# A streaming-encoder block: conditioning vector summed from row blocks of its weights, and a first FFN stage without the shift

## The chip, the core and the metric

The kernel runs on one core of a Trainium2 chip. The time is device microseconds of that core, from start to end of one execution. The core has TensorE (matmuls, written PE in the profile), VectorE (DVE), ScalarE (ACT), GpSimd (POOL) and SyncE (SP), which here only issues transfers. They run side by side and wait for each other by semaphores.

## The reference

A block of a network on x with 512 tokens of width 1024. A vector `ada` of 9 x 1024 numbers is made from the condition c; it gives a shift, a scale and a gate to each of three sublayers: a gated FFN, a mixer of 16 attention heads, and a second FFN.

```python
cond = jax.nn.silu(c)
ada = (cond @ w_ada[l] + b_ada[l]).reshape(b, N_SUBLAYERS, 3, D_MODEL)
shift, scale, gate = ada[:, :, 0], ada[:, :, 1], ada[:, :, 2]
h = modulate(x, g_ffn1[l], shift[:, 0], scale[:, 0])   # rmsnorm(x, g) * (1 + scale) + shift
x = x + 0.5 * gate[:, 0][:, None, :] * swiglu(h, w_ffn1_up[l], w_ffn1_down[l])
...
# swiglu(h, w_up, w_down): gate, up = split(h @ w_up); (silu(gate) * up) @ w_down
```

All is float32: x is 2 MB, `w_ada` is 37.7 MB (1024 x 9216), an FFN has 2816 hidden columns.

## The kernel before

The width of 1024 is 8 chunks of 128 rows (`KC`), on the partitions. A weight tile is 1024 rows by 128 columns, 512 KB. Precise products are made of three matmuls: each operand is split in a high part (rounded, by ScalarE: `split_hi`, `split_first`) and a low part (the remainder, by VectorE: `split_lo`, `split_first_lo`), and `three` adds high x high, high x low and low x high. So h is two tensors, `h_hi` and `h_lo`. A pair of up tiles (gate and up columns of the same 128 hidden ones) gives two PSUM banks; ScalarE takes silu of one, VectorE multiplies (`hidden`), and the product is split again.

**The start.** SP loads x in halves, eleven small vectors between the halves into `vecs`, and then sixteen column tiles of `w_ada` (shift and scale of the first sublayer, one by one for each chunk) with the first four up tiles among them. TensorE transposes x by chunks (L734); ScalarE copies and squares; VectorE sums the squares. A column of `ada` is made from a column tile in one of three ways (`ADA_ROLE`): by TensorE alone ("P": eight matmuls of one column, L712), or by a product with the condition on VectorE or GpSimd (L481), a reduce on VectorE (L1341) and one matmul with ones (L716). ScalarE adds the bias (L1069) and makes the factor `amp` (L1072). For each chunk k, VectorE normalises (L1372), ScalarE adds the shift and rounds (L1049), VectorE makes the low part (L1378), and TensorE then runs chunk k of all four first tiles (`first_tiles`, lines 688 to 690): the chunk can't start before its own shift and scale are there.

**The loop of FFN 1.** Twenty pairs, two tiles each (`up_pair`). With each pair two column tiles of `w_ada` are loaded into `ada_w`, multiplied on GpSimd (L481), reduced on VectorE (L1341) and summed over partitions on TensorE (L723). The down projection (8 output chunks) takes the last sixteen columns along.

**What sets the order.** Each engine has one queue, written by hand, and does its instructions in that order. A load of tile t waits until tile t - 4 has been split; the split of tile t waits until TensorE has used tile t - 2.

## Time and profile before

| | us |
|---|---|
| median of 3 runs | 1182.02 |
| lowest and highest | 1178.54, 1183.63 |
| span of the profiled execution | 1185.1 |
| TensorE busy in it | 1142.3 |
| VectorE, ScalarE, GpSimd busy | 650.4, 446.4, 188.5 |

The profile comes from one execution of its own. It has the busy time of every engine, the granted clock of TensorE, and for each instruction its start, its duration and what it waited for. A TensorE duration includes the pipeline's tail, so the step from one start to the next says what a matmul costs in a row of them. A float32 matmul of one column and a transpose are counted by instructions: a matmul of 128x1 has two of them.

### The profile page before, as it was taken

How to read it: one execution, taken by the hardware profiler on the slowest of the kernel's cores; microseconds unless marked ns; L12 is line 12 of the kernel's file. 1: busy time of each engine (PE TensorE's matmuls, PEld its weight loads, DVE VectorE, ACT ScalarE, POOL GpSimd, SP SyncE). 2: the span in 40 equal slices, each digit the busy share in tenths (PEclk: the TensorE clock that was granted, in tenths of full speed). 3: DMA queues.
4: the chain of work that ended last, by engine and by line, in shares of the span. 5: the costliest groups of instructions: out<-in, count | busy, mean ns of one | idle time of the engine just before them, and what ended most of it. 6: DMA issues, size and time to landing. Idle time of an engine off the chain costs nothing.

```text
span 1185.1 us, 14961 instructions
## 1 busy us (share of the span) xinstructions
PE 1142.3 (96%) x5249; PEld 915.5 (77%) x5249; DVE 650.4 (55%) x784; ACT 446.4 (38%) x748; POOL 188.5 (16%) x112
## 2 busy tenths in 40 slices
PE   7799999999999988999999999989999999999998
PEld 6678888888888865888778777777888888887876
DVE  3967676767665645566765566654333333334343
ACT  4233233232322224565676565343222222222322
POOL 2523333232322220000000000000000000225250
PEclk7699999999999998999999999999999999999999
DMA  9656666666675551112212111231333333223231
GB/s 272 156 146 175 190 172 190 173 187 168 166 183 149 149 150 36 54 54 54 54 53 64 44 36 54 61 101 52 89 96 99 88 88 100 86 72 107 83 104 71
DMA packets 231861, 131.20 MB, mean 111 GB/s; under 512 B 5148, under 2 KB 224396, under 8 KB 231820
## 3 DMA queue, kind: packets, MB, share of 16 engines
q1 hardware_dynamic: 231820, 130.66, 39.5%
q8 instruction: 25, 0.41, 0.1%
q14 instruction: 16, 0.13, 0.0%
HBM read 128.54 MB, written 2.10 MB: 110 GB/s over the span
## 4 chain that ended last, share of the span: by engine, by line
PE 89%; DVE 5%; ACT 2%; issue 1%; SPq 1%; DMA 1%; POOL 0%; DVEq 0%; ACTq 0%; POOLq 0%
PE bank L688 29%; PE bank L690 27%; PE bank L689 27%; PE bank L904 1%; PE bank L929 1%; DVE w_lo L1333 1%; PE bank L884 1%; DVE h_lo L1378 1%; DVE tmp L1372 1%; DVE ada_acc_first L1341 1%; ACT w_hi L1019 1%; SPq L608 1%; PE bank L723 1%; DMA ada_first<-in_w_ada_dram 1%; DVE w_lo L1383 1%
## 5 line engine op out<-in xcount | busy, mean ns | idle before, releaser
L1333 DVE TENSOR_TENSOR w_lo<-w_raw,w_hi 128x1024 fp32r<-128x1024 f32 x164 | 225.5, 1376 | 368.9 <-ACT w_hi L1019 367.8
L688 PE MATMUL bank<-h_hi,w_hi 128*128 128x512 f32 x864 | 353.7, 409 | 12.5 <-DVE h_lo L1378 8.0
L1019 ACT ACTIVATE w_hi<-w_raw 128x1024 fp32r<-128x1024 f32 x164 | 173.7, 1059 | 463.8 <-PE bank L690 448.3
L690 PE MATMUL bank<-h_hi,w_lo 128*128 128x512 f32 x864 | 345.0, 399 | 0.0
L689 PE MATMUL bank<-h_lo,w_hi 128*128 128x512 f32 x864 | 345.0, 399 | 0.0
L688 PEld LDWEIGHTS bank<-h_hi,w_hi 128*128 128x128 f32 x864 | 164.8, 191 | 55.2 <-DVE h_lo L1378 8.4
L689 PEld LDWEIGHTS bank<-h_lo,w_hi 128*128 128x128 f32 x864 | 164.8, 191 | 40.1 <-issue 2.6
L690 PEld LDWEIGHTS bank<-h_hi,w_lo 128*128 128x128 f32 x864 | 164.4, 190 | 40.1
L580 POOL TENSOR_TENSOR w_raw<-w_raw,gate_row 128x1024 f32<-128x1024 f32 (+1 forms) x24 | 54.9, 2287 | 662.8 <-DMA w_raw<-in_w_ffn_down_dram 662.4
L481 POOL TENSOR_TENSOR ada_w<-ada_w,cond 128x1024 f32<-128x1024 f32 x57 | 110.2, 1934 | 263.6 <-DMA ada_w<-in_w_ada_dram 263.4
L1341 DVE TENSOR_REDUCE ada_acc<-ada_w 128x128 f32<-128x1024 f32 x56 | 111.7, 1995 | 0.0
L688 PE MATMUL bank<-w_hi,hid_hi 128*128 128x512 f32 x176 | 70.4, 400 | 3.0 <-DVE w_lo L1333 3.0
L688 PE MATMUL bank<-hid_hi,w_hi 128*128 128x512 f32 x176 | 71.1, 404 | 0.3 <-DVE w_lo L1333 0.3
L690 PE MATMUL bank<-hid_hi,w_lo 128*128 128x512 f32 x176 | 69.7, 396 | 0.0
L689 PE MATMUL bank<-hid_lo,w_hi 128*128 128x512 f32 x176 | 69.7, 396 | 0.0
L690 PE MATMUL bank<-w_hi,hid_lo 128*128 128x512 f32 x176 | 69.4, 395 | 0.0
L689 PE MATMUL bank<-w_lo,hid_hi 128*128 128x512 f32 x176 | 69.0, 392 | 0.0
L1445 DVE TENSOR_TENSOR hid_lo<-tmp_b,hid_hi 128x512 f32 (+1 forms) x44 | 41.4, 946 | 36.3 <-ACT hid_hi L1105 36.3
L1105 ACT ACTIVATE hid_hi<-tmp_b 128x512 f32 (+1 forms) x44 | 27.8, 632 | 77.9 <-DVE tmp_b L1441 77.9
L1638 DVE TENSOR_TENSOR_SCAN tmp_b<-tmp_a,tmp_b 128x512 f32<-128x512 f32 (+3 forms) x32 | 25.1, 815 | 36.7 <-ACT tmp_a L1253 36.7
L688 PEld LDWEIGHTS bank<-w_hi,hid_hi 128*128 128x128 f32 x176 | 33.0, 188 | 11.4 <-DVE w_lo L1333 3.9
L690 PEld LDWEIGHTS bank<-w_hi,hid_lo 128*128 128x128 f32 x176 | 33.0, 188 | 8.5
(185 smaller groups left out, 1430.6 us busy)
## 6 DMA issues: line engine op xcount, KB each, us to landing
w_raw<-in_w_ffn_up_dram SPq DMA_DIRECT2D x88, 512.0 KB, 4.5
ada_w<-in_w_ada_dram SPq DMA_DIRECT2D x60, 512.0 KB, 3.9
w_raw<-in_w_ffn_down_dram SPq DMA_DIRECT2D x36, 512.0 KB, 4.6
w_raw<-in_w_in_dram SPq DMA_DIRECT2D x28, 512.0 KB, 3.9
ada_first<-in_w_ada_dram SPq DMA_DIRECT2D x12, 512.0 KB, 7.4
w_raw<-in_w_out_dram SPq DMA_DIRECT2D x8, 512.0 KB, 3.7
w_raw<-in_w_ffn_down_dram SPq DMA_DIRECT2D x8, 384.0 KB, 5.3
x_nat<-in_x_dram SPq DMA_DIRECT2D x2, 1024.0 KB, 5.2
```

Source lines behind the costliest of these rows:

```text
L481: return engine.tensor_tensor(tile, tile, cond[:].rearrange("p (k o) -> p k o", o=1) .broadcast_to([P, KC, P]), ALU.mult)
L580: g.tensor_tensor(tile, tile, gate_row[:, :, half * 512:(half + 1) * 512] .broadcast_to([P, nk, 512]), ALU.mult).then_inc(w_gated, 1)
L608: sp.dma_start(stage(p), ada_v[:, :, a * P:(a + 1) * P]).then_inc(ada_first_in[p], 16)
L688: mm(dst, wh, xh, start=start, stop=False, skip_group_check=skip)
L689: mm(dst, wh, xl, start=False, stop=False, skip_group_check=skip)
L690: return mm(dst, wl, xh, start=False, stop=stop, skip_group_check=skip)
L1019: a(w_hi[:, s, :], w_raw[:, r, :], ACT.Copy).then_inc(w_hi_done, 1)
L1105: a(hid_hi[:, bass.ds(f, 1), :], tmp_b[:, j:j + 1, :], ACT.Copy).then_inc(hid_hi_done, 1)
L1333: v.tensor_tensor(w_lo[:, s, :], w_raw[:, r, :], w_hi[:, s, :].bitcast(F32), ALU.subtract)\
L1341: return v.tensor_reduce(acc, tile.rearrange("p k n -> p n k"), AX_X, ALU.add).then_inc(ada_red, 1)
L1445: v.tensor_tensor(hid_lo[:, bass.ds(f, 1), :], tmp_b[:, j:j + 1, :], hid_hi[:, bass.ds(f, 1), :].bitcast(F32), ALU.subtract).then_inc(hid_ ...
L1638: last = v.tensor_tensor_scan(buf[:, back], tmp_a[:, unit % 2, back], buf[:, back], 0.0, ALU.add, ALU.add)
```

## The change

The vector `ada` is now made by row blocks. A block is one of the nine 1024-column parts; for each chunk k of 128 rows, the 128 x 1024 piece is loaded, 4 KB to a partition.

- **Scale of the first sublayer.** Its eight pieces come first, behind x. TensorE makes it alone: `ada_direct`, eight matmuls of one column for each piece, placed between the transposes and behind the sum of squares. With the last three stand matmuls on constants whose result nobody reads (`warm`: 2, 2, and 12).
- **The first four tiles without shift.** h is first xT * rstd * amp (`raw_high`, `raw_low`), and the four tiles run on this, tiles 0 and 1 ahead of 2 and 3 for the first chunks, and then as pairs (`first_pair`).
- **Shift.** Its eight pieces come behind the four weight tiles. VectorE multiplies by the condition and adds up (`shift_product`, one operation a piece), and TensorE sums over partitions (`ada_columns`, eight matmuls). The shift's part of the four tiles is a product of the unsplit weights with the shift: `shift_bias`, 32 matmuls of one column in two runs. It joins as a bias in `silu_first` and `hidden_first`.
- **h with shift** is made afterwards (`scaled`, `make_h_first`, `h_low_first`) over the same `h_hi`, `h_lo`, for tile 4 on.
- **The other seven blocks.** Five in the up loop, one for four pairs, two in the down projection. VectorE does `block_product` (one operation a piece, eight a block), TensorE `ada_columns` once a block, VectorE the bias (`ada_sum`). GpSimd has no part in it any more.
- The eleven small loads go out on ScalarE's queue. The first two weight tiles have buffers of their own. The stationary operand of the forget gate is packed.

```diff
@@ sync
             load_x(0)
-            sp.wait_ge(vec_zero, 1)
...
             load_x(1)
-            for p in range(ADA0):
-                load_ada_first(p)
-                if p in (3, 7):
-                    load_up(0, T_UP1, p // 4, p // 4, True)
+            load_first_block(B_SCALE, 0, scale_in)
+            for n in range(4):
+                load_up_first(n)
+            load_first_block(B_SHIFT, 1, shift_in)
...
+            with sp.Fori(0, UP_BLOCKS) as i:
+                for q in range(4):
+                    if q == 1:
+                        sp.wait_ge(bias_summed, 2)
+                    load_up(0, T_UP1, 4 * i + 2 + q, q % 2)
+                    if q % 2:
+                        sp.wait_ge(w_used, 4)
+                        for k in range(2 * q - 2, 2 * q + 2):
+                            load_ada(i + B_LOOP, k)
@@ tensor
+            def ada_direct(block, k, landed):
+
+                pe.wait_ge(landed[k], 16)
+                for j in range(KC):
+                    last = mm(bank[4][:, j:j + 1], ada_first[:, 1 - block, k, j * P:(j + 1) * P], cond[:, k:k + 1],
+                              start=k == 0 and j == 0, stop=k == KC - 1, skip_group_check=True)
+                if k == KC - 1:
+                    last.then_inc(ada_col, 1)
+
+            def ada_columns(products, read):
+
+                pe.wait_ge(ada_mul, products)
+                pe.wait_ge(ada_out, read)
+                for j in range(KC):
+                    last = mm(bank[4][:, j:j + 1], ada_acc[:, j * P:(j + 1) * P], ones[:], start=True, stop=True)
                 last.then_inc(ada_col, 1)
...
+            def warm(n):
+
+                for _ in range(n):
+                    mm(bank[3][:].rearrange("p (b n) -> p b n", n=P), ident_bf[:],
+                       ident_bf[:].rearrange("p (o n) -> p o n", o=1).broadcast_to([P, 4, P]), start=True, stop=True)
...
-                if k == KC - 2:
+                if k == 2:
                     pe.wait_ge(consts, N_CONSTS)
                     pe.wait_ge(cond_ready, 1)
-                    for p in range(2):
-                        ada_column_first(p)
+                if k >= 3:
+                    ada_direct(B_SCALE, k - 3, scale_in)
             sum_squares(0)
+            for k in range(KC - 3, KC):
+                ada_direct(B_SCALE, k, scale_in)
+                warm(2)
+            warm(10)
...
+            def first_pair(f, k):
+
+                pe.wait_ge(raw_done, k + 1)
+                for n in (2 * f, 2 * f + 1):
+                    last = tile_chunk(T_UP1, n, k, w2_hi, w2_lo)
...
+            def shift_bias(f):
+
+                for n in (2 * f, 2 * f + 1):
+                    for k in range(KC):
+                        raw = tile8(w_first[n], 0) if n < 2 else tile8(w_raw, n)
+                        last = mm(bank[6 + f][:, n:n + 1], raw[:, k, :], ada[:, k:k + 1], start=n % 2 == 0 and k == 0,
+                                  stop=k == KC - 1, skip_group_check=True)
+                last.then_inc(bias_summed, 1)
+
+            for n in range(2):
+                for k in range(3):
+                    pe.wait_ge(raw_done, k + 1)
+                    tile_chunk(T_UP1, n, k, w2_hi, w2_lo)
+            for k in range(3):
+                first_pair(1, k)
+            for k in range(3, KC):
+                first_pair(0, k)
+            for k in range(3, KC):
+                first_pair(1, k)
+                if k == 4:
+                    ada_columns(KC, B_SCALE)
+                if k > 5:
+                    if k == 6:
+                        pe.wait_ge(ada_out, 2)
+                    shift_bias(k - 6)
@@ vector
+            def block_product(block, k):
+
+                dve.wait_ge(ada_in[k % 2], 64 * block + 16 * (k // 2) - 112)
+                ada_product(k, ada_w[:, k % 2, :], KC * block + k - KC)
...
+            def hidden_first(f):
+
+                dve.wait_ge(bias_summed, f + 1)
+                v.tensor_copy(first_bias[:, 2 * f:2 * f + 2], bank[6 + f][:, 2 * f:2 * f + 2]).then_inc(bias_col, 1)
+                dve.wait_ge(bias_col, f + 1)
```

Two places show how the order moves. The first is TensorE's queue at the program's start, before the change (L734 transposes x, L712 and L716 are columns of `ada`, L699 and L701 the sum of squares, L688 to L690 the first tiles):

```order
L734 MATMUL bank<-ident,x_nat 128x128 x20
L712 MATMUL bank<-cond,ada_w 128x1 x16
L734 MATMUL bank<-ident,x_nat 128x128 x4
L699 MATMUL bank<-ssum,ones 128x512
L701 MATMUL bank<-tmp_a,ones 128x512
L712 MATMUL bank<-cond,ada_first 128x1 x8
L716 MATMUL bank<-ones,ada_acc_first 128x1
L712 MATMUL bank<-cond,ada_first 128x1 x8
L716 MATMUL bank<-ones,ada_acc_first 128x1
L688 MATMUL bank<-h_hi,w_hi 128x512
```

And with it (L707 transposes, L680 is `ada_direct`, L671 and L673 the sum of squares, L696 is `warm`):

```order
L707 MATMUL bank<-ident,x_nat 128x128 x4
L680 MATMUL bank<-cond,ada_first 128x1 x8
L707 MATMUL bank<-ident,x_nat 128x128 x4
L680 MATMUL bank<-cond,ada_first 128x1 x8
L671 MATMUL bank<-ssum,ones 128x512
L673 MATMUL bank<-tmp_a,ones 128x512
L680 MATMUL bank<-cond,ada_first 128x1 x8
L696 MATMUL bank<-ident_bf 128x512 x2
L680 MATMUL bank<-cond,ada_first 128x1 x8
L696 MATMUL bank<-ident_bf 128x512 x2
L680 MATMUL bank<-cond,ada_first 128x1 x8
L696 MATMUL bank<-ident_bf 128x512 x12
```

The transposes and direct groups alternate five times (the last two are shown), and three more groups with `warm` stand between the sum of squares and the first tile.

The second is TensorE at the end of the four first tiles (L755 is `shift_bias`, L789 the head of the loop). Before, the loop followed the last L690 of the tiles; now:

```order
L755 MATMUL bank<-ada,w_first_87 128x1 x8
L755 MATMUL bank<-ada,w_first_88 128x1 x8
L660 MATMUL bank<-h_hi,w_hi 128x512
L661 MATMUL bank<-h_lo,w_hi 128x512
L662 MATMUL bank<-h_hi,w_lo 128x512
L660 MATMUL bank<-h_hi,w_hi 128x512
L661 MATMUL bank<-h_lo,w_hi 128x512
L662 MATMUL bank<-h_hi,w_lo 128x512
L755 MATMUL bank<-ada,w_raw 128x1 x16
L789 UNCONDITIONAL_BRANCH
```

Two runs of sixteen matmuls of one column, 32 instructions each, have come in, with one chunk of tiles 2 and 3 between.

## Rows read from the trace of the kernel before

**Rows 1.** The page: busy time, the chain that ended last, a load's landing
```profile
PE 1142.3 (96%) x5249; PEld 915.5 (77%) x5249; DVE 650.4 (55%) x784; ACT 446.4 (38%) x748; POOL 188.5 (16%) x112
...
PE 89%; DVE 5%; ACT 2%; issue 1%; SPq 1%; DMA 1%; POOL 0%; DVEq 0%; ACTq 0%; POOLq 0%
...
w_raw<-in_w_ffn_up_dram SPq DMA_DIRECT2D x88, 512.0 KB, 4.5
```
**Rows 2.** Windows: stretch, length, busy us (count) by engine, clock, DMA, GB/s
```profile
13.20:16.00 2.80, 2.80 (x28) 2.80 (x27) 1.55 (x3) 1.34 (x3) 0.00 (x0) 1.00 1.16 290
...
21.50:28.80 7.30, 7.30 (x35) 7.23 (x33) 1.93 (x3) 4.49 (x10) 1.90 (x1) 0.50 1.17 292
...
56.90:58.80 1.90, 1.90 (x19) 1.90 (x18) 1.86 (x2) 0.00 (x0) 0.00 (x0) 1.00 0.00 0
71.30:73.60 2.30, 0.14 (x2) 0.01 (x1) 2.30 (x3) 1.17 (x3) 2.12 (x2) 1.00 1.19 294
74.10:77.40 3.30, 3.30 (x9) 2.53 (x9) 3.30 (x5) 0.70 (x2) 0.60 (x1) 0.50 0.10 26
100.00:200.00 100.00, 100.00 (x446) 81.19 (x445) 70.79 (x53) 30.48 (x51) 32.29 (x17) 1.00 0.64 179
```
**Rows 3.** Timeline of TensorE, 6 to 79 us: start, duration, instruction, idle before
```profile
6.06 1.94 PE L734 MATMUL bank<-ident,x_nat 128*128 128x128 f32 x8 [6.06 <-DMA x_nat<-in_x_dram]
...
12.64 0.66 PE L734 MATMUL bank<-ident,x_nat 128*128 128x128 f32 x4 [0.32 <-ACT tmp_a L1032]
13.13 4.20 PE L712 MATMUL bank<-cond,ada_w 128*128 128x1 f32 x32
17.20 1.09 PE L734 MATMUL bank<-ident,x_nat 128*128 128x128 f32 x4
18.08 1.91 PE L699 MATMUL bank<-ssum,ones 128*128 128x512 f32 x2
...
21.50 3.41 PE L712 MATMUL bank<-cond,ada_first 128*128 128x1 f32 x16
...
34.81 0.80 PE L688 MATMUL bank<-h_hi,w_hi 128*128 128x512 f32 x1 [5.37 <-DVE h_lo L1378]
35.40 0.63 PE L689 MATMUL bank<-h_lo,w_hi 128*128 128x512 f32 x1
35.83 0.63 PE L690 MATMUL bank<-h_hi,w_lo 128*128 128x512 f32 x1
...
71.04 0.39 PE L690 MATMUL bank<-h_hi,w_lo 128*128 128x512 f32 x1
73.59 0.51 PE L688 MATMUL bank<-h_hi,w_hi 128*128 128x512 f32 x1 [2.16 <-DVE tmp_b L1441]
...
78.04 0.40 PE L688 MATMUL bank<-h_hi,w_hi 128*128 128x512 f32 x1
78.28 0.40 PE L689 MATMUL bank<-h_lo,w_hi 128*128 128x512 f32 x1
```
**Rows 4.** Timeline of ScalarE: the first table load, a weight split
```profile
0.74 1.28 ACT L1026 ACT_TABLE_LOAD   x1 [0.74 <-PEq L1712]
...
31.37 1.06 ACT L1078 ACTIVATE w_hi<-w_raw 128x1024 fp32r<-128x1024 f32 x1 [1.16 <-DMA w_raw<-in_w_ffn_up_dram]
```
**Rows 5.** Timeline of SyncE's queue: the small loads' first issue, x's second half
```profile
1.25 0.51 SPq L622 DMA_DIRECT2D vecs<-in_b_ada_dram  x1
...
5.00 0.41 SPq L611 DMA_DIRECT2D x_nat<-in_x_dram  x1
```
**Rows 6.** Timeline of VectorE: the condition's last step, h low, weight low, product
```profile
10.33 0.17 DVE L1412 TENSOR_TENSOR cond<-cond,vcol 128x8 f32<-128x8 f32 x1
...
38.35 0.73 DVE L1378 SCALAR_TENSOR_TENSOR h_lo<-tmp,ada,h_hi 128x512 fp32r<-128x512 f32 x1
39.01 1.21 DVE L1383 TENSOR_TENSOR w_lo<-w_raw,w_hi 128x1024 fp32r<-128x1024 f32 x1
...
42.00 1.21 DVE L481 TENSOR_TENSOR ada_first<-ada_first,cond 128x1024 f32<-128x1024 f32 x1
```

More of the change, by code:

```diff
@@ L24 @@
 EPS = 1e-6
-N_IDENT, N_CONSTS = 2, 15
+N_IDENT, N_CONSTS = 4, 15
 NEG = -(2.0 ** 126)
@@ L30 @@
 NADA = 9 * KC
-ADA0 = 2 * KC
-ADA_ROLE = "PPPGPGPG" "GDGGPGDG"
-ADA_DOWN = ADA0 + 2 * (FC - 2)
-ADA_SUMS = [p for p in range(ADA0) if ADA_ROLE[p] != "P"]
+NBLOCK = 9
+B_SHIFT, B_SCALE, B_LOOP = 0, 1, 2
+UP_BLOCKS = (FC - 2) // 4
+DOWN_CHUNKS = (3, 3, 2, 0)
 T_UP1 = 0
@@ L778, in up_pair @@
                     last.then_inc(w_used, 1)
[L779 to L785 removed]
+            with pe.Fori(0, UP_BLOCKS) as i:
+                for q in range(4):
+                    up_pair(T_UP1, 4 * i + 2 + q, q % 2, 0, q == 0)
+                ada_columns(KC * i + 2 * KC, i + B_LOOP)
             pe.wait_ge(hid_done, FC - 1)
@@ L1097, in up_chunk @@
                         a(tmp_a[:, j, :], bank[j][:], ACT.Silu).then_inc(silu_done, 1)
-                if with_ada:
-                    for half in range(2):
-                        ada_bias(ADA0 - 4 + 2 * f + half, half)
                 hidden_high(f, j, hid0)
@@ L1295, in _ @@
             make_h(2)
-            ffn_up(T_UP2, FC, False)
+            nc.scalar.preload_act_table_set("silu_and_others")
+            split_hi(T_UP2 + 2 * SPLIT, used=T_UP2)
+            for j in range(2):
+                act.wait_ge(w_used, T_UP2 + 2 * j + 1)
+                a(tmp_a[:, j, :], bank[j][:], ACT.Silu).then_inc(silu_done, 1)
+            split_hi(T_UP2 + 2 * SPLIT + 1, used=T_UP2 + 1)
+            for j in range(2):
+                hidden_high(j, j, FC)
+            with act.Fori(1, FC // 2 - 1) as i:
+                for j in range(2):
+                    up_chunk(T_UP2, 2 * i + j, j, FC)
+            for j in range(2):
+                up_chunk(T_UP2, FC - 2 + j, j, FC)
             def square_out(half, tb):
@@ new lines, in hidden_low @@
+            def hidden_low(f, j, hid0):
+                dve.wait_ge(hid_hi_done, hid0 + f + 1)
+                v.tensor_tensor(hid_lo[:, bass.ds(f, 1), :], tmp_b[:, j:j + 1, :],
+                                hid_hi[:, bass.ds(f, 1), :].bitcast(F32), ALU.subtract).then_inc(hid_done, 1)
+            dve.wait_ge(rstd_done, 1)
+            for k in range(KC):
+                v.tensor_tensor(xr[:, k, :], xT[:, k, :], rstd[:], ALU.mult).then_inc(xr_done, 1)
+            ada_sum(B_SCALE, 1)
+            dve.wait_ge(ada_out, 1)
@@ new lines, in _ @@
+            v.scalar_tensor_tensor(amp[:], ada[:, KC:2 * KC], 1.0, col(R_G[0], KC), ALU.add, ALU.mult).then_inc(amp_done, 1)
+            dve.wait_ge(amp_done, 1)
+            dve.wait_ge(xr_done, KC)
+            raw_low(0)
+            split_up(0)
+            raw_low(1)
+            split_up(1)
+            raw_low(2)
+            raw_low(3)
+            split_up(2)
+            raw_low(4)
+            split_up(3)
+            raw_low(5)
+            shift_product(0)
+            raw_low(6)
@@ new lines, in _ @@
+            shift_product(1)
+            raw_low(7)
+            for k in range(2, KC):
+                shift_product(k)
+            ada_sum(B_SHIFT, 2)
+            dve.wait_ge(ada_out, 2)
+            scaled(0)
+            for k in range(1, 4):
+                scaled(k)
+                h_low_first(k - 1)
+            split_lo(2 * SPLIT)
+            scaled(4)
+            h_low_first(3)
+            hidden_first(0)
+            scaled(5)
+            h_low_first(4)
+            split_lo(2 * SPLIT + 1)
@@ L1436, in hidden @@
+            for k in range(6, KC):
+                scaled(k)
+                h_low_first(k - 1)
+            h_low_first(KC - 1)
+            hidden_low(0, 0, 0)
+            hidden_first(1)
+            hidden_low(1, 1, 0)
             def hidden(base, f, j, hid0, first=False):
@@ L1678, in _ @@
             split_first_lo(T_UP2 + 2, w3_hi, w3_lo)
-            coefficients(2, 9 * KC)
+            coefficients(2)
             normed(2)
-            ffn_up(T_UP2, FC, False)
+            split_lo(T_UP2 + 2 * SPLIT)
+            for j in range(2):
+                hidden(T_UP2, j, j, FC, True)
+            split_lo(T_UP2 + 2 * SPLIT + 1)
+            for j in range(2):
+                hidden_low(j, j, FC)
+            with dve.Fori(1, FC // 2) as i:
+                for j in range(2):
+                    f = 2 * i + j
+                    for half in range(2):
+                        split_lo(T_UP2 + 2 * f + half + SPLIT, half, (2 * j + half + SPLIT) % RAW)
+                    hidden(T_UP2, f, j, FC)
+                    hidden_low(f, j, FC)
             for t in range(T_DOWN2 + SPLIT, T_DOWN2 + len(NAT_PARTS) + SPLIT):
```

401 lines of the change are left out of this document (175 added, 226 removed).

## The prediction, made before the changed kernel was run

> **What bounds the kernel now.** I read the page first, then the TensorE row of time in the first 90 us, then what the other engines and the DMA do in the same stretch. The page shows TensorE busy 96% of the span and 89% of the chain that ended last is TensorE's [rows 1], so only stretches where TensorE idles, runs at the half clock or does small extra matmuls can change the time. From 100 to 200 us, inside the up loop, it is busy without a break at the full clock, with 64% of the DMA's share in use [rows 2]; the loops are its own time. The losses are at the start, and the change works there.
>
> In that start the reader is to see five things. The first transposes start at 6.06, the first matmul of the up tiles at 34.81, the last of the four first tiles at 71.04 and the first of the loop at 73.59 [rows 3]: the 96 matmuls of the first tiles spread over 36.5 us. A 128x512 matmul follows the one before it by 0.43 us at the half clock (35.40 to 35.83) and by some 0.233 at the full one (78.04 to 78.28) [rows 3]; 96 are 22.4 us at full. The granted clock was 1.00 (2.4 GHz) up to 16.0, 0.50 (1.2 GHz) behind it, 1.00 again at 56.9, and 0.50 once more from 74.1 to 77.4, behind the idle 71.3 to 73.6 [rows 2]. A 128x1 matmul is two instructions: 19 in 1.9 us at full (56.9 to 58.8), 35 in 7.3 at half (21.5 to 28.8) [rows 2], so eight matmuls, 16 instructions, are 1.7 and 3.3. And TensorE was busy with little else for all of 13.2 to 16.0 and 21.5 to 28.8; right behind the first the clock was lost, and in the second it did not come back [rows 2, 3].
>
> **The change, part by part.** I follow TensorE's new order.
>
> Start to the third transpose group. x's second half is no longer behind eleven small loads on SP; these go out on ScalarE's queue once its table is loaded at 2.02 [rows 4]. Eleven issues took from 1.25 to 5.0 on SP [rows 5], so on ScalarE they would end near 5.8, before its first copy, which waits for the transposes of 6.06 [rows 3]. The vector of conditions is ready at 10.5 before (VectorE at 10.33) [rows 6]. I take 10.6 again; if the small loads are late behind x and the weights, each microsecond counts. TensorE then does the fourth group of transposes: 11.2.
>
> The scale block on TensorE. Eight groups of 16 instructions (ada_direct) stand there, against six such in the whole start before. Bounds: 1.7 each at full, 3.3 at half. The first two I take at full (before, the same mix kept the full clock to 16.0, [rows 2]); from then on half. Sum: 11.2 + 1.7 + 0.6 + 1.7 = 15.2; three groups of transposes at 0.9 (17.20 to 18.08; 0.6 at full, 12.64; [rows 3]) and three direct groups at 3.3: 27.8; sum of squares 3.4 (18.08 to 21.50, [rows 3]): 31.2; two direct groups and two matmuls of warm each, 0.43 apiece: 39.5; the last: 42.8; twelve of warm, 5.1: 47.9. The normalisation by rstd (eight VectorE operations of 0.7) lies under this. So do the loads: x and scale are 6.3 MB, at the 290 GB/s of the 512 B pieces [rows 2] 22 us, and the last of the block is wanted at 39.5.
>
> The first four tiles. Behind the last direct group come a sum, the coefficient, h's high part (0.7), its low part (0.7), and the first weight split (1.06 on ScalarE, 1.2 on VectorE) [rows 4, 6], about 4.5 us: under the twelve of warm. Then VectorE alternates h chunks and splits, with the third h chunk at about 49.6 and the fourth split at 53.2; TensorE keeps close behind. I add 1.2 us for that and for the first matmuls at the half clock (bounds 0 and 3). 90 of the 96 matmuls are 21.0, the eight columns of shift 1.7: 47.9 + 1.2 + 21.0 + 1.7 = 71.8. The shift products (eight at about 1.2, nearest row the 1.21 us product at 42.00 [rows 6]) end near 65, the shift block has landed by about 45 even at 290 GB/s; both hidden. That is a stretch of 24 us where before it took 36.5: this is what the change gains, from a start that is 13 us later.
>
> The bias. shift_bias gives TensorE 64 new instructions of 128x1 work, in two runs of 32, with 6 large matmuls between: 3.4 + 1.4 + 3.4 = 8.2 at full, 16.4 at half. Before, such a run began at 13.13 and the clock was gone 2.9 us later [rows 2, 3]. With the same 2.9 here, it goes at 74.7, and the 5.3 us that are left take 10.6: 85.3. The loop then starts at the half clock; before, this cost nine matmuls 0.2 each, 1.8 us (74.1 to 77.4, [rows 2]), and I take 1.8 again. Expressed as if at full, the loop starts at 87.1; before, at 73.59 + 1.8 = 75.4. **The sum is +11.7 us.**
>
> The rest of the work on h. scaled and h_low_first stand on VectorE behind the shift columns (69.0): eight of 0.4 to 0.7, eight of 0.7, two splits of 1.2, hidden_first: the last chunk at 82 to 85. TensorE reads it last in tile 4, after 92. Nothing, unless the loop starts ten microseconds sooner. The first loop weights (tile 4 and 5) are in by then, since tiles 0 and 1 end early; the idle 71.3 to 73.6 of before goes, and is counted above. Tile 6 waits on SP for the second bias and is wanted 6 us later or more; a load takes 4.5 [rows 1].
>
> The loops. GpSimd's product and VectorE's reduce of each tile become one VectorE operation of about 1.2 [rows 6], and TensorE waited for neither, being busy all of the 100 us [rows 2]. TensorE's columns were four instructions a pair and become 16 after four pairs: 1.7 us either way. SP now waits inside a block for products; the nearest deadline is a weight tile issued after a product some 3.6 us into a tile step and wanted 11.3 us after that step began; with its two predecessors it lands at about 9. Two microseconds of slack: 0.
>
> I weigh one rule here. The row: after transposes from 6.06 on, the clock stood at 1.00 until 16 [rows 2, 3]. The Trainium skill, TensorE: Matmul & The Clock Gate, Part 4, says that transposes do not count as activity for the clock. By it the two first direct groups would be at half too, and the sum 4 us more. The durations in the row (four transposes in 0.66 before 13.3, in 1.09 at 17.20) speak for full [rows 3], and I keep that.
>
> **Rivals.**
> A. The clock stays at full through the 128x1 work, since TensorE is busy. Then the direct groups save 6 x 1.6, the transposes 0.7, the sum of squares 1.7, the warm ones 3.4, so 15 us, of which VectorE's splits give back about 2; and the bias stays at 8.2: the loop starts at 67, 8.4 us earlier than before: 1173.6. Against it stands 21.5 to 28.8, all busy at 0.50 [rows 2]. The Trainium skill, same page, Part 1, says that the clock follows how busy TensorE has been, which read plainly is this rival; the trace disagrees for this kind of matmul. Chance 0.09.
> B. The direct groups are at half, but the bias is not hit, because large matmuls stand before, between and after: loop at 80.0, +4.6, so 1186.6. For it: 1.9 us of 128x1 at 56.9 left the clock at 1.00 [rows 2]. Against: the runs here are 3.4. Chance 0.15.
> C. The columns of a block in the loops, now 1.8 us in one run, cost the clock too. Seven places at 1.8: 12.6 more, 1206. Against: the same 1.9 us at 56.9. Chance 0.06.
> D. My forecast, with its own range +6 to +18 (clock lost at 13 or at 19 in the start, 4 us; first tiles 0 or 3; bias hit at once or late, 3). Chance 0.70.
>
> **How the numbers follow.** The span of the profiled execution is 1185.1, the median of the runs 1182.0; the sum is made in the first and added to the second: 1182.0 + 11.7 = 1193.7. The range 1184 to 1203 leaves out A and C and takes in B. A difference of 0.5%, 5.9 us, is about what a measurement of this kernel can tell from none. Faster by more: A, 0.09. Within: B and the low edge of D, 0.19. Slower: the rest, 0.72.
>
> **What would show it.** In the profile after: granted clock 0.50 from about 15 to 48 with the direct groups at 3.3 us each and the last ending near 43; the first large matmul at 47 to 49; the four tiles to the first bias in 24 us; the clock at 0.50 again during the second bias run and over the first matmuls of the loop, which starts at 83 to 87; the loops as before. It is wrong if the clock is at 1.00 in the direct groups, if the second bias run takes 3.4 us, or if TensorE waits in the loop for weights.

## The result, and the profile after

The changed kernel took **1195.36 us** (median of four runs, 1190.83 to 1195.76), the kernel before beside it 1182.16 us (1178.54 to 1183.63): a ratio of **1.0105, 95% interval 1.0079 to 1.013**, slower by 13.2 us. Run once more beside other kernels later (after_again, below), it took 1192.86 us, a ratio of 1.0085 (1.0065 to 1.0104). The profiled execution has a span of 1193.3 us.

First the page of the changed kernel, the lines that answer to [rows 1]: busy time, the chain that ended last, the landing of an up tile and of a 128 x 1024 piece of `w_ada`.

```profile
PE 1158.9 (97%) x5357; PEld 932.6 (78%) x5357; DVE 583.5 (49%) x808; ACT 438.3 (37%) x676; POOL 61.7 (5%) x48
...
PE 94%; DVE 3%; ACT 1%; DMA 0%; issue 0%; ACTq 0%; DVEq 0%
...
w_raw<-in_w_ffn_up_dram SPq DMA_DIRECT2D x86, 512.0 KB, 3.8
ada_w<-in_w_ada_dram SPq DMA_DIRECT2D x56, 512.0 KB, 3.5
```

TensorE's busy time rose from 1142.3 to 1158.9 us, VectorE's fell from 650.4 to 583.5 and GpSimd's from 188.5 to 61.7. The work has been moved off the engines with room and onto the one that bounds the kernel, whose part of the chain went from 89 to 94%.

Now TensorE's timeline of the start, which answers to [rows 3] (start, duration, instruction, idle before it and what ended it):

```profile
10.37 0.47 PE L713 MATMUL bank<-ident,vecs 128*128 128x128 f32 x1 [2.39 <-DMA vecs<-in_g_fox_k_dram]
...
12.14 1.09 PE L707 MATMUL bank<-ident,x_nat 128*128 128x128 f32 x4 [0.45 <-issue]
13.02 3.41 PE L680 MATMUL bank<-cond,ada_first 128*128 128x1 f32 x16
...
17.18 3.41 PE L680 MATMUL bank<-cond,ada_first 128*128 128x1 f32 x16
...
44.65 3.41 PE L680 MATMUL bank<-cond,ada_first 128*128 128x1 f32 x16
47.92 4.51 PE L696 MATMUL bank<-ident_bf 128*128 128x512 bf16 x12
52.19 0.48 PE L660 MATMUL bank<-h_hi,w_hi 128*128 128x512 f32 x1
...
76.02 4.26 PE L755 MATMUL bank<-ada,w_first 128*128 128x1 f32 x32
...
82.84 6.82 PE L755 MATMUL bank<-ada,w_raw 128*128 128x1 f32 x32
89.53 0.77 PE L660 MATMUL bank<-h_hi,w_hi 128*128 128x512 f32 x1
```

The reader is to see three stretches. All eight direct groups (L680) take 3.41 us, 3.28 from the start of one to what follows it: half clock from the first one on. The first large matmul stands at 52.19, where it stood at 34.81. From it to the first bias column (L755) are 23.8 us, and from there to the head of the loop at 89.53 are 13.5 us, in two runs: 4.1 us, nearly all at full clock, and 6.7 us at half, with 2.7 us of large matmuls between. Before, the loop's head stood at 73.59.

The windows that answer to [rows 2] (stretch, length, busy us and count of PE, PEld, DVE, ACT, POOL, granted clock, DMA share, GB/s):

```profile
13.20:16.00 2.80, 2.80 (x16) 2.80 (x14) 1.11 (x3) 1.08 (x2) 0.00 (x0) 1.00 1.03 410
21.50:28.80 7.30, 7.30 (x38) 7.30 (x36) 1.38 (x2) 2.17 (x4) 0.00 (x0) 1.00 1.13 340
76.10:78.90 2.80, 2.80 (x28) 2.80 (x26) 2.80 (x5) 2.28 (x3) 0.00 (x0) 0.99 0.01 3
82.90:89.50 6.60, 6.60 (x33) 6.60 (x32) 4.80 (x8) 2.26 (x4) 0.00 (x0) 0.50 0.00 0
100.00:200.00 100.00, 100.00 (x447) 81.18 (x446) 50.85 (x55) 27.58 (x34) 0.00 (x0) 1.00 0.63 186
```

Here the clock column misleads. It reads 1.00 in the first two windows, but 16 instructions in 2.80 us against 28 in the window of the same 2.80 us at 76.10 show that TensorE ran at half there. Up to the first fall of the clock that it shows, in this trace at 78.9, the column says 1.00 whatever went before; the length of a shape that stands at both levels decides. The same holds for the kernel before, where the column reads 1.00 up to 16.0 [rows 2]: its first eight transposes took 1.94 us, and four took 0.66 at 12.64 [rows 3], so the clock was at half at 6.06 and rose in between. The last row is as before (446 instructions in 100 us): the loops did not change.

### The profile page after: what moved, and what is told of

It reads as the page before. It is cut to its first block, busy times and chain, and to the rows that moved or that the text cites. A ratio compares the mean times of both kernels' runs of the same rounds, so it can differ in the third digit from the quotient of the medians.

```text
span 1193.3 us, 14658 instructions
## 1 busy us (share of the span) xinstructions
PE 1158.9 (97%) x5357; PEld 932.6 (78%) x5357; DVE 583.5 (49%) x808; ACT 438.3 (37%) x676; POOL 61.7 (5%) x48
## 3 DMA queue, kind: packets, MB, share of 16 engines
q1 hardware_dynamic: 167136, 130.60, 36.1%
## 4 chain that ended last, share of the span: by engine, by line
PE 94%; DVE 3%; ACT 1%; DMA 0%; issue 0%; ACTq 0%; DVEq 0%
PE bank L660 29%; PE bank L662 28%; PE bank L661 28%; PE bank L680 2%; PE bank L912 1%; PE bank L937 1%; PE bank L690 1%; PE bank L755 1%; PE bank L890 1%; DVE w_lo L1357 1%; ACT w_hi L1027 1%; PE bank L707 0%; DVE h_lo L1407 0%; PE bank L970 0%; DMA vecs<-in_g_fox_k_dram 0%; PE bank L673 0%
## 5 line engine op out<-in xcount | busy, mean ns | idle before, releaser
L1357 DVE TENSOR_TENSOR w_lo<-w_raw,w_hi 128x1024 fp32r<-128x1024 f32 x164 | 218.2, 1331 | 412.0 <-ACT w_hi L1027 411.7
L660 PE MATMUL bank<-h_hi,w_hi 128*128 128x512 f32 x864 | 349.5, 405 | 3.8 <-DVE h_lo L1407 2.0
L1370 DVE SCALAR_TENSOR_TENSOR ada_acc<-ada_w,cond,ada_acc 128x1024 f32<-128x1024 f32 x49 | 62.7, 1280 | 0.0
L1482 DVE TENSOR_TENSOR hid_lo<-tmp_b,hid_hi 128x512 f32 (+1 forms) x44 | 30.4, 693 | 36.9 <-ACT hid_hi L1124 36.9
L662 PEld LDWEIGHTS bank<-hid_hi,w_lo 128*128 128x128 f32 x176 | 33.0, 188 | 8.1
L661 PEld LDWEIGHTS bank<-hid_lo,w_hi 128*128 128x128 f32 x176 | 33.0, 188 | 8.0
```

Source lines behind the costliest of these rows:

```text
L660: mm(dst, wh, xh, start=start, stop=False, skip_group_check=skip)
L661: mm(dst, wh, xl, start=False, stop=False, skip_group_check=skip)
L662: return mm(dst, wl, xh, start=False, stop=stop, skip_group_check=skip)
L1357: v.tensor_tensor(w_lo[:, s, :], w_raw[:, r, :], w_hi[:, s, :].bitcast(F32), ALU.subtract)\
L1370: ins = v.scalar_tensor_tensor(ada_acc[:], source, cond[:, k:k + 1], ada_acc[:], ALU.mult, ALU.add)
L1482: v.tensor_tensor(hid_lo[:, bass.ds(f, 1), :], tmp_b[:, j:j + 1, :], hid_hi[:, bass.ds(f, 1), :].bitcast(F32), ALU.subtract).then_inc(hid_ ...
```

## The experiments

TensorE's timeline of the profiled execution of each kernel gives four milestones, and the runs the time (the ratio is to the kernel before on the same chip, whose median lay between 1182.2 and 1183.5 us each time; "half from" gives the time at which the granted clock fell just at or behind the head):

| kernel | first large matmul | first bias column | loop head | clock at the head | time, us | ratio (95%) |
|---|---|---|---|---|---|---|
| before | 34.81 | none | 73.59 | half from 74.0 | 1182.2 | |
| after | 52.19 | 76.02 | 89.53 | half | 1195.4 | 1.0079 to 1.013 |
| after_again | 49.62 | 72.96 | 85.36 | half | 1192.9 | 1.0065 to 1.0104 |
| small_loads_on_sp | 48.01 | 71.40 | 79.86 | half from 79.9 | 1188.7 | 1.0038 to 1.0089 |
| no_bias | 49.03 | 72.39 | 77.92 | half | 1185.5 | 1.0015 to 1.0052 |
| scale_on_vector | 34.84 | 58.66 | 72.22 | half | 1179.8 | 0.9958 to 0.9995 |
| bias_spaced | 51.90 | 75.69 | 88.03 | full | 1191.4 | 1.006 to 1.0109 |
| bias_between | 49.20 | 71.43 | 84.40 | half | 1196.0 | 1.0091 to 1.0128 |
| direct_spaced | 58.47 | 82.26 | 95.84 | half | 1202.8 | 1.0115 to 1.0184 |
| spaced_from_full | 42.86 | 66.68 | 76.71 | half from 77.0 | 1185.1 | 1.0004 to 1.0038 |
| bias_single | 52.52 | 73.77 | 86.44 | full | 1189.8 | 1.0036 to 1.0078 |
| no_warm | 50.39 | 74.88 | 84.91 | half from 85.1 | 1192.6 | 1.0052 to 1.0098 |
| combined | 33.44 | 56.11 | 70.27 | half | 1177.6 | 0.994 to 0.9968 |
| combined_single | 33.90 | 55.36 | 68.02 | full | 1172.9 | 0.9885 to 0.9941 |

My theory at the outset: the 13 us are TensorE's 128x1 matmuls, in two places, each doubled by the half clock. Eight direct groups (26 us) stand ahead of the first tiles, and the bias (11 us without the large matmuls between) ahead of the loop. The rivals were other waits (the small loads, VectorE's chain of h) and a clock that is low for another reason.

### Is it the scale block on TensorE? (scale_on_vector)

```
-                if k >= 3:
-                    ada_direct(B_SCALE, k - 3, scale_in)
             sum_squares(0)
-            for k in range(KC - 3, KC):
-                ada_direct(B_SCALE, k, scale_in)
-                warm(2)
-            warm(10)
+            ada_columns(KC, 0)
+            warm(12)
...
+            def scale_product(k):
+                dve.wait_ge(scale_in[k], 16)
+                ada_product(k, ada_first[:, 0, k, :], k)
```

> The changed kernel, but the scale block is made as the shift is: eight products on VectorE between its sums of squares, then eight one-column matmuls, then the twelve warm ones. The direct groups are gone from TensorE. My theory is that these, at the half clock, set the start: 26.6 us of direct groups go, 3.3 of columns come. VectorE's products would end near 26, the columns at 29.5, the coefficient at 31, the first large matmul at 35 to 36 instead of 52.2. The rest as it is: 16 us less, 1179. Rival: the pieces' landing sets the start, not TensorE: the last piece would land past 30 and the gain is under 10 us, 1186 or more. Rival: VectorE is late, since normalising x now queues behind the products: 12 us less, 1183.

It took 1179.81 us, ratio 0.9976 (0.9958 to 0.9995), as expected: this term alone is 13 us against after_again and 15.5 against after, and decides the sign. Its TensorE rows of the stretch:

```profile
19.30 1.13 PE L671 MATMUL bank<-ssum,ones 128*128 128x512 f32 x2 [2.24 <-DVE ssum L1434]
...
26.07 3.58 PE L690 MATMUL bank<-ones,ada_acc 128*128 128x1 f32 x16 [4.10 <-DVE ada_acc L1366]
...
34.84 0.47 PE L660 MATMUL bank<-h_hi,w_hi 128*128 128x512 f32 x1 [0.32 <-DVE w_lo L1462]
```

One run of 16 instructions takes the place of eight; TensorE waits 2.24 and 4.10 us for VectorE, and still the first large matmul stands 17.4 us earlier. Seven of the eight products cost VectorE 1.2 us each and the first 0.7, at a time when it had nothing else: in the changed kernel it idled 10.5 us ahead of the operations on rstd and 5.1 us ahead of the coefficient.

```profile
38.10 4.90 DVE L1487 TENSOR_TENSOR xr<-xT,rstd 128x512 f32<-128x512 f32 x8 [10.54 <-ACT rstd L1054]
48.10 0.17 DVE L1386 TENSOR_TENSOR ada<-bank,vcol 128x8 f32<-128x8 f32 x1 [5.10 <-PE bank L680]
```

### What is the bias worth, and what hides behind it? (no_bias)

```
-                    for k in range(KC):
+                    for k in (0,):
                         raw = tile8(w_first[n], 0) if n < 2 else tile8(w_raw, n)
```

> Leaves out 28 of the 32 one-column matmuls of the shift's bias (one for each tile stays, so that the order and the waits are the same); the first two hidden chunks then lack most of the shift. By my account the two runs and the chunk between them took 13.5 us, and the half clock at the head of the loop 1.2 more. With four matmuls and one chunk left, about 2.3 us, TensorE reaches the loop near 78.5 instead of 89.5. The cover over VectorE's chain on h goes then: its last chunk was ready at 87.2, and would be at 85 to 86 without the waits for the bias, where TensorE wants it at 83.5. So 10 to 11 us less in all, 1185. Rival: the clock is not part of it, and the bias costs only its 6.8 us at full: 1189. Rival: h is the real bound there, and TensorE waits 5 us or more for it: 1190.

This kernel leaves out 28 of the 32 columns, so its first two hidden chunks lack most of the shift; it is there to price them. 1185.45 us, as expected, 7 to 10 us less than the changed kernel, where the bias took 13.5. The row at the loop's head says why not all of it comes back:

```profile
77.92 0.80 PE L660 MATMUL bank<-h_hi,w_hi 128*128 128x512 f32 x1 [3.19 <-DVE tmp_b L1477]
```

With the columns gone TensorE waits for VectorE's hidden tile, which had lain beside them.

### Is the second run long by the half clock? (bias_spaced)

```
                         last = mm(bank[6 + f][:, n:n + 1], raw[:, k, :], ada[:, k:k + 1], ...)
+                        if n % 2 == 0 or k < KC - 1:
+                            mm(bank[5][:]..., ident_bf[:], ..., start=True, stop=True)
```

> The changed kernel with a large matmul on constants behind each one-column matmul of the bias (30 in all, result unused). If the half clock is what doubles the second bias run (6.7 us against 4.1), spacing keeps the clock at 1.00: the runs cost 6.8 us of columns and 30 x 0.23 of large ones, 13.7, plus 1.4 for the chunk between, and the loop starts at the full clock: about 15.1 against 13.5 + 1.2, so within 1 us of the changed kernel, 1196, with the granted clock at 1.00 throughout. Rival: the second run is slow for its own sake (another weight buffer, transfers beside it): then its columns still take 6.7 and all large ones come on top, 1202 or more.

The clock was kept, from before the bias to the loop and beyond:

```profile
60.00:90.00 30.00, 30.00 (x186) 25.92 (x185) 22.33 (x32) 9.57 (x13) 0.00 (x0) 1.00 0.01 4
```

and 30 matmuls of 128x512 more made the stretch shorter: 12.3 us from the first bias column to the loop head for 13.5. The pairs are cheaper than I expected, 0.353 us (75.69 to 76.04 in the timeline), hence 1191.44 and not 1196 us. So neither the buffer nor the weight load makes the second run long; in the next kernel both runs stand at full clock, and each takes 3.5 us to what follows it.

### The small loads (small_loads_on_sp)

```
             load_x(0)
+            (the eleven small loads, sp.dma_start in place of act.dma_start)
             load_x(1)
```

> The changed kernel with the eleven small loads back on SyncE's queue, between the halves of x. In the changed kernel TensorE waited 2.4 us for the last of them, the condition was ready at 12.05 instead of 10.5, and every transpose and direct group ran at the half clock. My theory: the 2.4 us gap in TensorE's transposes also cost it the full clock that the kernel before had from its first transposes to 16.0. Then the wait goes (1.5 us on the path), the transposes of 10.4 on take 0.66 a group and the first one or two direct groups 1.7 instead of 3.3: 4 to 5 us less, 1190 to 1191. The rival, that transposes don't raise the clock: only the 1.5 us, 1194, with direct groups of 3.3 from the first on.

1188.74 us, below both. The mechanism was the rival's all the same: the vector came without a wait and the first direct group began at 11.51 for 13.02, but at half clock, as did every transposition. In its profiled execution, the fastest of its five runs (1185.85 us), the rest of the gain came from somewhere else, as the rows behind the sum of squares and at the bias show:

```profile
34.98 2.13 PE L687 MATMUL bank<-cond,ada_first 128*128 128x1 f32 x16
...
37.40 1.95 PE L687 MATMUL bank<-cond,ada_first 128*128 128x1 f32 x16
...
40.02 3.41 PE L687 MATMUL bank<-cond,ada_first 128*128 128x1 f32 x16
...
71.40 3.63 PE L762 MATMUL bank<-ada,w_first 128*128 128x1 f32 x32
76.38 3.63 PE L762 MATMUL bank<-ada,w_raw 128*128 128x1 f32 x32
```

The clock was at full for some 3 us behind the sum of squares and fell again, and both bias runs were at full: it fell only at 79.9, 8.5 us after the first bias column. The first of these two events is no effect of the edit, as the next run shows. Whether the edit has a part in the second is open: the same instructions stand there, but the five runs have a median 4.9 us below that of the changed kernel's eight, and one profile was taken. What the trace shows for the edit itself is the 1.5 us at the first direct group.

### The changed kernel again (after_again)

> The changed kernel as it is, beside the others of this call: 1195 us, first large matmul at 52 us, two bias runs of 4.1 and 6.7 us. If the place of TensorE's clock changes from one execution to the next (small_loads_on_sp met both bias runs at full clock), the second bias run may be of 3.5 us here and the time 2 to 3 us less.

```profile
36.35 1.84 PE L680 MATMUL bank<-cond,ada_first 128*128 128x1 f32 x16
...
72.96 3.63 PE L755 MATMUL bank<-ada,w_first 128*128 128x1 f32 x32
78.68 6.82 PE L755 MATMUL bank<-ada,w_raw 128*128 128x1 f32 x32
```

The same program had here the 3 us at full clock behind the sum of squares that it had not in its first profile, and so its first large matmul at 49.62 for 52.19. The eight runs of the changed kernel lie between 1190.8 and 1195.8 us, with a median of 1193.7, 11 us over the kernel before. The moving clock is a likely reason for part of that spread, but it is not shown: two of the eight were profiled, and the kernel before spreads as far (1178.3 to 1188.0 in 23 runs).

### Does a column between large matmuls keep the clock? (bias_between, bias_single)

bias_between puts two or three columns behind each of the last 12 large matmuls; bias_single makes the sum of the shift one chunk earlier, puts one column behind each of the last 18, and then alternates the 14 that are left with large matmuls of constants (shortened; the loop at the end is bias_single's alone):

```
-                    shift_bias(k - 6)
+                    for m in range(6):
+                        big = mm(... the m-th large matmul of chunk k ...)
+                        bias_column()        # three (two) of them in bias_between
...
+            while bias_cols:
+                bias_column()
+                if bias_cols:
+                    mm(bank[5][:]..., ident_bf[:], ..., start=True, stop=True)
```

> The changed kernel, but the 32 column matmuls of the bias stand two or three at a time behind each of the last 12 large matmuls of the third and fourth tile, instead of in two runs of 16. Clock theory (a run of 128x1 matmuls costs TensorE its clock, large ones among them keep it, as in bias_spaced): the stretch from the first bias column to the loop head keeps the full clock, the columns add 4.5 to 7 us in place of 13.5, the loop head's 1.2 us go, and some 2 us come back as a wait for VectorE's h, which no_bias showed to be next: 1187 us. Rival (the columns themselves cost 0.42 us each wherever they stand): 1195 us.

> The changed kernel, but the columns of the shift follow the fourth piece of the third and fourth tile instead of the fifth, and then one bias column matmul stands behind each of the last 18 large matmuls, and the 14 that are left stand each before a large matmul of constants. Theory (what counts is how dense the large matmuls stand: one large per column keeps the clock, as in bias_spaced; three columns per large lose it after 6 us, as in bias_between): full clock from the first bias column to the loop head, 32 pairs of 0.353 us there = 11.3 us of which 18 large matmuls (4.2 us) would run anyway: 7.1 us for 13.5, loop head at about 82 to 83 us at full clock for 89.5 at half, no or little wait there for VectorE: 1187 us, and 1188 at most if the start is one of the longer ones. Rival (VectorE's h and hidden chain is next): a wait of 3 us or more at the loop head, 1190 us or over.

bias_between brought nothing (1196.03 us; three runs of four lie at 1195.9 to 1196.2, and the profiled one is the fourth, at 1190.9). With two or three columns to a large matmul the clock held for 6 us and then fell in the middle of the stretch, which took 13.0 us for 13.5. A pair of rows at either level:

```profile
72.02 0.47 PE L757 MATMUL bank<-h_lo,w_hi 128*128 128x512 f32 x1
72.33 0.72 PE L766 MATMUL bank<-ada,w_first 128*128 128x1 f32 x6
...
78.42 0.77 PE L757 MATMUL bank<-h_hi,w_lo 128*128 128x512 f32 x1
79.00 1.27 PE L766 MATMUL bank<-ada,w_raw 128*128 128x1 f32 x6
```

bias_single kept the clock to the loop's head at 86.44, with a start as late as the changed kernel's (52.52), and took 1189.75 us over ten runs:

```profile
73.91 0.48 PE L766 MATMUL bank<-h_lo,w_hi 128*128 128x512 f32 x1
74.22 0.28 PE L756 MATMUL bank<-ada,w_first 128*128 128x1 f32 x2
74.36 0.47 PE L766 MATMUL bank<-h_hi,w_lo 128*128 128x512 f32 x1
...
83.61 0.38 PE L803 MATMUL bank<-ident_bf 128*128 128x512 bf16 x1
83.82 0.28 PE L756 MATMUL bank<-ada,w_raw 128*128 128x1 f32 x2
86.44 0.48 PE L660 MATMUL bank<-h_hi,w_hi 128*128 128x512 f32 x1
```

It is 2.7 us worse than expected, and here is why: behind a large matmul of the tile a pair takes 0.453 us (73.91 to 74.36), with one of constants 0.353. 18 times 0.1 are 1.8 us of the 2.7. VectorE's chain was no bound; TensorE nowhere waits for it at the head.

### Can spacing bring the clock, or only keep it? (direct_spaced, spaced_from_full)

```
                               start=k == 0 and j == 0, stop=k == KC - 1, skip_group_check=True)
+                    warm(1)
...
                     pe.wait_ge(consts, N_CONSTS)
+                    warm(4)                  # spaced_from_full alone, with the small loads on SP
                     pe.wait_ge(cond_ready, 1)
```

> The changed kernel, but behind each of the 64 column matmuls of the scale block stands one large matmul of constants (128x512 bf16). Clock theory (it is the shape of the 128x1 matmuls and the transpositions that keeps TensorE at half clock there, and 512 columns among them raise it; a pair at full clock takes 0.353 us, by bias_spaced): direct groups of 2.8 us for 3.28, transpositions of 0.55 us for 1.09 and the 12 warm matmuls of 2.8 us for 4.5, first large matmul 6 to 9 us earlier: 1187 to 1189 us, and the clock event that now stands at 51.9 us stands before 20 us. Rival (the clock is low there for another reason, as the time since the start or what the core did before): the pairs take 0.84 us, each group 6.7 us: over 1215 us.

> direct_spaced with two edits ahead of it: the small loads on SP's queue, and four large constant matmuls in TensorE's wait for the condition. In direct_spaced pairs of a column matmul and a large one started at half clock and stayed there for 30 us, until the sum of squares; in bias_spaced the same pairs started at full clock and kept it. Theory (such pairs keep the clock that is there but do not bring it; transpositions that run without a gap and the four matmuls bring it, as it stood at full from 11 us in combined): clock up at 11 to 12 us and kept, pairs of 0.353 us, groups of 2.8 us, transpositions of 0.55 us, last direct group ends near 37 us for 48, first large matmul near 41 to 44 us: 1184 to 1187 us. Rival (the first 40 us are at half for a reason of their own): pairs of 0.667 us as in direct_spaced, 1200 us.

My theory fell with direct_spaced: 1202.81 us (three runs of four at 1202.8 to 1205.0, one at 1194.5). The pairs began at half clock and stayed there for 30 us, at 0.67 us each; the clock rose only at 44.0, in the sum of squares, where large matmuls follow each other:

```profile
12.62 0.43 PE L680 MATMUL bank<-cond,ada_first 128*128 128x1 f32 x2
12.91 0.59 PE L697 MATMUL bank<-ident_bf 128*128 128x512 bf16 x1
13.29 0.42 PE L680 MATMUL bank<-cond,ada_first 128*128 128x1 f32 x2
```

The corrected theory, that such pairs keep a full clock but do not bring it, was what spaced_from_full tested. Four large matmuls in the wait for the condition are its only other new work; the small loads are on SP's queue:

```profile
9.11 1.91 PE L704 MATMUL bank<-ident_bf 128*128 128x512 bf16 x4
10.81 1.06 PE L715 MATMUL bank<-ident,x_nat 128*128 128x128 f32 x4
11.67 0.42 PE L687 MATMUL bank<-cond,ada_first 128*128 128x1 f32 x2
11.96 0.46 PE L704 MATMUL bank<-ident_bf 128*128 128x512 bf16 x1
12.26 0.28 PE L687 MATMUL bank<-cond,ada_first 128*128 128x1 f32 x2
```

The clock rose at 12 and stayed through all eight groups, 2.8 us each. The first large matmul stands at 42.86, and the time is 1185.13 us, within the 1184 to 1187 expected. Apart from the four matmuls TensorE's work and order are those of direct_spaced; 17.7 us lie between them, of which the trace puts about 1.5 down to the small loads. That the four brought the clock is not shown apart from the small loads: in combined, with the same loads and without the four, the clock was at full at 10.44 too. For them speaks that all ten runs lie between 1183.1 and 1186.6 us.

### The constant matmuls (no_warm)

```
                 ada_direct(B_SCALE, k, scale_in)
-                warm(2)
-            warm(10)
```

> The changed kernel without its 16 large constant matmuls behind the direct groups. Theory: four of them stand on the path (the last direct group ends 1.7 us earlier and with it VectorE's and ScalarE's work on the factor), the other 12 stand in TensorE's wait for VectorE and cost nothing, but bring the clock: without them the first large matmul stands at about 50.5 us for 52.2 and the first tiles run at half clock for 4 to 7 us, which costs half of that, 2 to 3.5 us: 1195 to 1197 us. Rival (they bring nothing, the clock rises by itself with the first tiles at the same time): 1193.5 us.

1192.55 us, below both expectations and within the spread of the changed kernel (1190.8 to 1195.8). What they were thought to bring is there: the first large matmul comes 1.8 us sooner (50.39) and nine of them run at half clock, 0.43 us apart, up to 54.4. What is lost there came back later in this execution: the clock fell 3.4 us after the first bias column, was back at full 3.4 us later and stood there during nearly all of the second bias run (3.88 us for 6.82), so that the stretch took 10.0 us for 13.5. So the 16 constant matmuls are worth nothing that can be measured here.

### Put together (combined, combined_single)

combined is scale_on_vector, small_loads_on_sp and bias_between in one; combined_single has bias_single's placing in place of bias_between's.

> The changed kernel with three of the edits together: the scale block summed on VectorE (scale_on_vector), the small loads on SP's queue, and the bias columns between the large matmuls (bias_between). If the three terms are independent: 1179.8 less 1 to 2 us for the small loads (in scale_on_vector TensorE still waits 1.77 us for them) less 6 to 8 us for the bias: 1172 us, below the kernel before by 10 us. Rival (VectorE's chain from the shift to the hidden tiles is next and takes the gain of the bias back, as the 3.19 us in no_bias): 1178 us.

> combined with the placing of bias_single in place of that of bias_between. In combined the clock fell 4.6 us after the first bias column, the loop head stood at 70.27 us at half clock. Theory: loop head at 65.5 to 66.5 us at full clock, 5 to 6 us less than combined: 1172 us. Rival (VectorE next): 1175 us or over.

combined took 1177.63 us, near its rival's 1178, but not for the rival's reason: TensorE did not wait for VectorE, the clock fell 4.5 us after the first bias column, and bias_between's gain was missing as in bias_between itself. combined_single took **1172.92 us, ratio 0.9913 (0.9885 to 0.9941)**, 9 us less than the kernel before and 20 to 22 less than the changed one. Its loop head came at 68.02 rather than 66, by the same 0.1 us in 18 pairs. So the rearrangement can gain; in the changed kernel it was spent on where its small matmuls were put.

## Why the prediction was right, and which of its steps were not

1193.7 us was predicted, 1195.36 measured; the two measurements of the changed kernel, +13.2 and +9.8 us, lie on either side of the predicted +11.7. The mechanism was right: 128x1 matmuls at half clock, in the start and at the bias. With a few microseconds between executions of one kernel, so close a hit is in part chance; the first step below was off by 5 us. Step by step, against the profile of after:

- **Start to the last direct group: wrong by 5.1 us**, 42.8 predicted, 47.9 measured. Two steps of it failed. The small loads were late, which I had named and put at nothing. Their issues on ScalarE's queue ran from 1.04 to 5.37, earlier than the 5.8 I had worked out, yet TensorE waited for them until 10.37, while the DMA was full of x and weights (1.05 of its share and 394 GB/s from 5.0 to 10.4). The condition's last step shows what that made of the 10.33 in [rows 6], and the first direct group began at 13.02 for 11.2:

```profile
11.88 0.17 DVE L1441 TENSOR_TENSOR cond<-cond,vcol 128x8 f32<-128x8 f32 x1
```

And "the first two I take at full" was wrong: 3.28 us each, not 1.7, and 0.3 us on the transposition between: 3.5 us. I had carried over the clock of 13.13 [rows 3] to another order of work, and read the column's 1.00 as full from 6.06 on. What keeps it at half there is open: in small_loads_on_sp, with TensorE idle for 1.16 us in place of 2.39, it was at half too, and in combined, with 1.15 us idle at the same place, at full. With four large matmuls there it was at full in the one kernel that had them (spaced_from_full).
- **Twelve constant matmuls: 4.3 us, predicted 5.1**, because the clock rose among them.
- **First tiles and shift columns: 23.8 us, predicted 23.9.** The 1.2 us taken for VectorE was one wait of 0.72 and half a microsecond of matmuls spaced wider.
- **The bias: 13.5 us, predicted 13.5,** and lost where it was said, 2.9 us in. This hit was in part luck: in the profiles with such runs the clock went 2.7 to 8.5 us after the first bias column, which is 13.5 (after) to 8.5 us (small_loads_on_sp) for the stretch; in no_warm and spaced_from_full it went 3.4 and 3.5 us in, came back 3.4 us later, and the stretch took 10.0 us. My range for D had this ("hit at once or late, 3"), a little too narrow.
- **h with the shift: last chunk at 87.2, predicted 82 to 85,** and hidden as predicted: TensorE did not wait for it.
- **The loop's head: 1.2 us, predicted 1.8:** six matmuls at half clock (89.53 to 92.2) for nine. In after_again they were twelve, 2.4 us.
- **The loops: about nothing, as predicted.** From the loop head to the second sublayer's rstd are 367.3 us (367.6 in after_again), 368.7 before.

The profiled execution of after thus has its loop head, with the half clock behind it counted, 15.3 us later than before (90.7 against 75.4), where 11.7 was predicted; after_again has it 12.4 us later (85.36 + 2.4). At the second sublayer's rstd, behind the loops, the two are 14.5 and 10.6 us later than before, near the medians' 13.2 and 9.8. The difference of the spans of before and after is only 8.2 us, because the profiled execution of before took 736.6 us from that rstd to its last matmul, and after 730.2. All thirteen traces of the changed kernel and its variants have 730.1 to 732.5 us there. I take the difference for that one execution's: its span of 1185.1 is above the times of all four runs beside it (1178.5 to 1183.6); that the change saves something there is not excluded, since a second trace of the kernel before is missing.

Of the rivals, A (full clock through the 128x1 work of the start) is in no trace where this work stands in unbroken runs; the most there is are some 3 us at full behind the sum of squares (after_again). B (the bias is not hit) is an outcome of single executions: small_loads_on_sp had it, no_warm and spaced_from_full half of it. C (the loops' columns cost the clock) did not happen: in after the granted clock is 1.00 from 92.6 to 454.0, over all seven blocks.

The rule on transposes that I weighed and set aside gave the better sum here for the two groups (its 4 us against 3.5 measured), but not by its mechanism. In the kernel before, eight transposes took 1.94 us at 6.06 [rows 3], the next eight 1.64, and four 0.63 behind them. In combined nothing but transposes ran up to 17.9 us, and between the four at 8.17, which took 1.12 us, and the eight at 10.44, which took 1.07, the clock rose.

```profile
8.32 1.64 PE L734 MATMUL bank<-ident,x_nat 128*128 128x128 f32 x8
10.78 0.63 PE L734 MATMUL bank<-ident,x_nat 128*128 128x128 f32 x4 [0.81 <-ACT tmp_a L1032]
```

```profile
8.17 1.12 PE L714 MATMUL bank<-ident,x_nat 128*128 128x128 f32 x4
10.44 1.07 PE L714 MATMUL bank<-ident,x_nat 128*128 128x128 f32 x8 [1.15 <-DVE cond L1463]
```

combined_single has the same instructions up to there and stayed at half (its groups of eight at 10.45 and 12.71 took 1.94 and 2.10 us); what decides between the two is open. The Trainium skill, TensorE: Matmul & The Clock Gate, Part 4, says that transposes do not count as activity for the clock; the traces of before and of combined disagree, 1.07 us for eight standing against 1.94.

## What to carry over

A long run of 128x1 matmuls costs TensorE its clock although it is never idle: price such a run at full clock up to where the clock goes (2.7 to 8.5 us in, here) and at twice that behind it, and what follows it at half too for some microseconds. If the columns must be on TensorE, put one behind each large matmul, which held a full clock in bias_spaced, bias_single, combined_single and spaced_from_full, and have the clock up before they start; if another engine idles at that time, sum there and leave TensorE one run of columns. When part of a start is moved, do not carry the clock over from the old trace: give both levels a price.

## What was unexpected

- Pairs of a 128x1 matmul (two instructions) and a 128x512 one hold the level of the clock that they meet: 0.353 us a pair over 25 us at full (spaced_from_full), 0.67 us a pair over 30 us at half (direct_spaced). What ran just before it rose in these two were large matmuls one behind the other, in spaced_from_full with four transposes behind them.
- When the clock changes differs between executions of one program: at the bias it fell 2.9 us (after), 4.1 (after_again) and, with the same instructions there, 8.5 us (small_loads_on_sp) after the first column, and behind the sum of squares it rose in one profile of the changed kernel and not in the other. One trace of such a start is therefore not enough. The Trainium skill, TensorE: Matmul & The Clock Gate, Part 1, says that the number of slow matmuls at a start varies from run to run of one kernel; the traces agree: in after TensorE's start is at half clock up to 51.5, in after_again it is at full from 36.1 to 39.5.
- The large row blocks arrive faster than the small pieces did: 410 GB/s in 13.2 to 16.0, where the kernel before had 290 in the same window [rows 2], with the DMA full in both (1.03 and 1.16 of its share). It paid nothing, since the weights were not what TensorE waited for; the small vectors, issued beside them on ScalarE's queue, were.
